# Down products ahead of the next up products in the first three places of a nine-unit expert round

## The reference, cut to what matters

```python
def expert_block(args):
    xb, e = args                       # up to 128 rows of one expert
    return (jax.nn.silu(xb @ w1[e]) * (xb @ w3[e])) @ w2[e]   # w1, w3: 1024x512, w2: 512x1024

y_rows = yb.reshape(-1, d)[dest] * wts.reshape(-1)[order][:, None]
return jnp.zeros_like(t).at[tok].add(y_rows)
```

## Time and profile before

| | us |
|---|---|
| median of 3 runs | 1163.68 |
| lowest, highest | 1163.40, 1164.49 |
| span of the profiled execution | 1160.8 |
| chain that ended last, by engine | PE 73%, DMA 14%, DVE 7%, ACT 3%, issue 2% |
| PE busy | 1093.8 (94% of the span) |
| DMA mean over the span | 241 GB/s |

### The profile page before, as it was taken

How to read it: one execution, slowest core, us unless ns; L and a number is a source line. 1 busy time by engine, 2 the same in 40 slices (tenths; PEclk the granted TensorE clock), 3 DMA queues, 4 the chain that set the end, 5 groups by cost and what they waited for, 6 DMA issues and landing times.

```text
span 1160.8 us, 16298 instructions
## 1 busy us (share of the span) xinstructions
PE 1093.8 (94%) x5691; PEld 700.4 (60%) x5691; DVE 562.6 (48%) x1011; ACT 317.0 (27%) x539; POOL 176.8 (15%) x255
## 2 busy tenths in 40 slices
PE   6999999989999999999999998899999899988985
PEld 4788888868667777778888777333333233322333
DVE  5776787745676788766564546221112111111114
ACT  4542322243334544342433242100000000000003
POOL 0000110000110323345000100122222122211220
PEclk9999999999999999999999998999999999999999
DMA  9423855720111222223132489989999999999975
GB/s 380 194 97 120 293 177 194 254 91 19 55 56 55 74 73 74 91 85 130 59 109 91 179 368 343 406 352 423 423 424 425 425 426 425 426 427 426 425 321 223
DMA packets 41981, 279.68 MB, mean 241 GB/s; under 512 B 7802, under 2 KB 8186, under 8 KB 30016
## 3 DMA queue, kind: packets, MB, share of 16 engines
q1 hardware_dynamic: 34496, 265.07, 57.3%
q0 software_dynamic: 7424, 13.80, 3.4%
HBM read 274.23 MB, written 13.40 MB: 248 GB/s over the span
## 4 chain that ended last, share of the span: by engine, by line
PE 73%; DMA 14%; DVE 7%; ACT 3%; issue 2%; SPq 0%; DVEq 0%; POOL 0%; ACTq 0%; POOLq 0%
PE psum L701 70%; DMA ering<-in_wb 8%; DMA ering<-in_wa 2%; DMA ada<-in_adaw 2%; DVE ring_lo L1538 1%; PE psum L717 1%; DVE amx L1809 1%; DVE sc L1798 1%; DMA xr<-token_rows,tabt 1%; ACT ring_hi L1235 1%; PE psum L1043 1%; PE psum L741 1%; DMA Hx<-in_xT 1%; DMA gat<-expert_rows 0%; ACT gth L1235 0%
## 5 line engine op out<-in xcount | busy, mean ns | idle before, releaser
L701 PE MATMUL psum<-ering,xs 128*64 128x512 f32 x1056 | 237.0, 599 | 18.7 <-DMA ering<-in_wb 9.1
L701 PE MATMUL psum<-Hhi,ring_hi 128*128 128x512 f32 x472 | 188.3, 399 | 0.1
L701 PE MATMUL psum<-Hlo,ring_hi 128*128 128x512 f32 x472 | 185.3, 393 | 0.2 <-DVE Hlo L1538 0.2
L701 PE MATMUL psum<-Hhi,ring_lo 128*128 128x512 f32 x472 | 183.1, 390 | 0.0
L701 PEld LDWEIGHTS psum<-ering,xs 128*64 128x64 f32 x1056 | 73.2, 137 | 160.9 <-issue 135.1
L1538 DVE TENSOR_TENSOR ring_lo<-ring,ring_hi 128x1024 fp32r<-128x1024 f32 x87 | 107.8, 1239 | 109.7 <-ACT ring_hi L1235 108.6
L1538 DVE TENSOR_TENSOR sg<-sg,psum 128x256 f32<-128x256 f32 x66 | 27.8, 421 | 236.8 <-ACT sg L1235 235.6
L701 PE MATMUL psum<-ering,at 128*64 128x512 f32 x528 | 119.5, 597 | 2.9 <-ACT at L1235 1.6
L1235 ACT ACTIVATE ring_hi<-ring 128x1024 fp32r<-128x1024 f32 x87 | 92.2, 1060 | 74.3 <-DMA ring<-in_stream 41.2
L701 PEld LDWEIGHTS psum<-Hhi,ring_hi 128*128 128x128 f32 x472 | 88.7, 188 | 22.7 <-issue 3.2
L701 PEld LDWEIGHTS psum<-Hhi,ring_lo 128*128 128x128 f32 x472 | 88.5, 188 | 19.7
(11 more groups left out here) (350 smaller groups left out, 1450.7 us busy)
## 6 DMA issues: line engine op xcount, KB each, us to landing
ering<-in_w SPq DMA_DIRECT2D x28, 2048.0 KB, 21.6
ering<-in_wb SPq DMA_DIRECT2D x28, 2048.0 KB, 27.8
ering<-in_wa SPq DMA_DIRECT2D x28, 2048.0 KB, 22.8
ring<-in_stream SPq DMA_DIRECT2D x87, 512.0 KB, 4.3
ada_ring<-in_stream SPq DMA_DIRECT2D x32, 512.0 KB, 3.7
ada<-in_adaw SPq DMA_DIRECT2D x4, 2048.0 KB, 10.8
Am<-decay_rows POOLq DMA_DIRECT2D x8, 512.0 KB, 4.5
gat<-expert_rows SPq DMA_DIRECT2D x4, 1024.0 KB, 8.0
```

The lines of the kernel that those rows point to most:

```text
L701: return nc.tensor.matmul(out, lhsT, rhs, start=start, stop=stop)
```

## The change

In the places with `a == 0` (q = 0, 1, 2) the test on `nh` goes, and `down`, `rows_out` and `rows_home_at` always stand ahead of the next unit's `up_and_gate`, `silu_times` and `gather`. The other six places, ScalarE and SyncE are as before.

```diff
--- before.py
+++ after.py
@@ -1194,8 +1194,11 @@
 
                                         up_and_gate(1, j, k + 1, here)
                                         tokens_in(1, k + 2)
-                                with pe.If(k >= nh):
+                                if a == 0:
                                     down(0, j, u + 1, here)
+                                else:
+                                    with pe.If(k >= nh):
+                                        down(0, j, u + 1, here)
                                 with pe.If(u + 1 < n):
 
                                     up_and_gate(0, (j + 1) % SLOTS, u + 2, then, True)
@@ -1206,10 +1209,11 @@
                                         act_turn(1, k + 1)
                                     with pe.If(u + 1 < n):
                                         tokens_in(0, u + 1)
-                                with pe.If(k < nh):
-                                    if heavy:
-                                        down(1, j, k + 1, here)
-                                    down(0, j, u + 1, here)
+                                if a > 0:
+                                    with pe.If(k < nh):
+                                        if heavy:
+                                            down(1, j, k + 1, here)
+                                        down(0, j, u + 1, here)
 
         for c in range(NCH):
             b = 4 + c % 2
@@ -2101,15 +2105,19 @@
                                     silu_times(1, k + 1)
                                     token_columns(1, k + 2)
                             with v.If(u < n):
-                                with v.If(k >= nh):
+                                if a == 0:
                                     rows_out(0, u + 1, u + 1)
+                                else:
+                                    with v.If(k >= nh):
+                                        rows_out(0, u + 1, u + 1)
                                 with v.If(u + 1 < n):
                                     silu_times(0, u + 2)
                                     token_columns(0, u + 1)
-                                with v.If(k < nh):
-                                    if heavy:
-                                        rows_out(1, k + 1, k + 1)
-                                    rows_out(0, u + 1, u + 1)
+                                if a > 0:
+                                    with v.If(k < nh):
+                                        if heavy:
+                                            rows_out(1, k + 1, k + 1)
+                                        rows_out(0, u + 1, u + 1)
 
         def rows_sum(c):
 
@@ -2263,15 +2271,19 @@
                                     with g_.If(k < nh):
                                         g_.wait_ge(xt_full[1], k + 2)
                                         gather(1, bass.ds(u * 2 + 2 * TRIO + 1, 1), k + 3)
-                                with g_.If(k >= nh):
+                                if a == 0:
                                     rows_home_at(0, bass.ds(u * 2, 1), u + 2)
+                                else:
+                                    with g_.If(k >= nh):
+                                        rows_home_at(0, bass.ds(u * 2, 1), u + 2)
                                 with g_.If(u + 1 < n):
                                     g_.wait_ge(xt_full[0], u + 1)
                                     gather(0, bass.ds(u * 2 + 6, 1), u + 2)
-                                with g_.If(k < nh):
-                                    if heavy:
-                                        rows_home_at(1, bass.ds(u * 2 + 1, 1), k + 2)
-                                    rows_home_at(0, bass.ds(u * 2, 1), u + 2)
+                                if a > 0:
+                                    with g_.If(k < nh):
+                                        if heavy:
+                                            rows_home_at(1, bass.ds(u * 2 + 1, 1), k + 2)
+                                        rows_home_at(0, bass.ds(u * 2, 1), u + 2)
 
     ctx.close()
```

## The result

The changed kernel takes 1168.53 us (median of 4 runs, 1167.96 to 1171.09), the kernel before 1163.54 beside it (4 runs, 1162.49 to 1164.49): 1.0056 times as long, interval [1.0041, 1.0072], 5.0 us slower by the medians, where +0.7 was forecast. The span of the profiled execution went from 1160.8 to 1166.1 us, +5.3.

A forecast was written before the change was run, and what follows sets the result against it. The expert stage was taken as bound by DMA, its weight stream; hole +0.5 and scatters +0.2 made span 1160.8 into 1161.5, so 1163.68 + 0.7 = 1164.4 us. The forecast's own range was 1163.3 to 1166.0, the overall range 1161.2 to 1167.7.

The forecast's parts named there:

- Scatters: In round 0, unit 1's eviction waits for unit 0's scatter, landing after 8.1 us, and delays unit 3's up: +0.2 (0 to 1.4).
- The late scatter as a rival: Unit 0's scatter lands late beside a full queue; at 11 us +3 and the hole +0.5, 1167.2 us; chance 0.11.
- the list of waits that the prediction counted: Eleven halves of up products on TensorE waiting for weight loads, 904.09 to 1060.28, taken to absorb PE's delay of rounds 1 and 2.
- The hole's own term: The early break in the weight stream moves back 10 us and lacks 5.4 to 6.0 against 5.2: +0.2 to +0.8, taken +0.5.
- slot 2's condition: Unit 5's `wa` and `wb` wait for unit 3's first up matmul, so go out at 766.17 instead of 761.17, taking the gain.
- three loads issued within a microsecond start faster: If these restart the stream after the hole faster than one load alone did, the low end of +0.2 to +0.8 is nearer.
- PE's delay: PE runs 4.0 us late in round 0 and 4.2 more in each of rounds 1 and 2; queued loads and waits absorb it.
- The reserve: Weight loads still queued at 817.33, the lowest point: 4.8 MB or 11 us, counting about 13 gathers and scatters; 4.0 fit.
- The gather: Now issued behind the scatter, near 762.8, landing at 770.9; `tokens_in` wants it at 771.9 with 0.8 us cover: costs nothing.
- Branches: A test and a code copy fall away at each changed place: taken as nothing, bounds -0.4 to 0.
- the ends -0.2 and +2.2: Lower and upper ends of the summed change, from +0.2 - 0.4 to +0.8 + 1.4, around the forecast +0.7.

The follow-up runs named there:

- run 3: The changed kernel with ten 128-column filler matmuls ahead of `act_turn` of unit 2 in round 0, shared buffer kept: 1166.17 us against 1162.31 for the kernel before.
- run 5: The changed kernel measured again, unaltered: 1167.52 us against 1162.22 for the kernel before.
- run 13: The changed kernel measured once more, unaltered, in the last set: 1169.22 us against 1162.78 for the kernel before.
- run 15: Down first in round 0 alone, shared buffer kept, without the third code copy: 1167.43 us against 1162.78 for the kernel before.
- run 1: The changed kernel with round 0 back in the old order, down first in rounds 1 and 2 only: 1163.06 us against 1162.31 for the kernel before.
- run 8: The kernel before with slot 2's wa and wb freed behind the up products at q = 0: 1161.82 us against 1162.22.
- run 12: The kernel before with a third copy of the code at q = 0 to 2, all in the old order: 1162.55 us against 1162.51.
- run 9: Down first in round 0 alone, unit 0's rows in their own buffer, no third code copy: 1163.93 us against 1162.51 for the kernel before.
- run 6: Down first in round 0 alone, unit 0's rows in their own buffer, with a third code copy: 1167.37 us, 1.0048 times the kernel before.
- run 2: The changed kernel with unit 0's rows in a buffer of their own: 1165.76 us against 1162.31 for the kernel before.
- run 7: Down first at q = 0 of round 0 only, own buffer, slot 2 freed early, third code copy there: 1167.62 us against 1162.22 for the kernel before.
- run 4: Down first in round 0 only, own buffer, slot 2 freed early, third code copy: 1168.39 us against 1162.31 for the kernel before.
- run 10: Run 9 with slot 2 freed early and GpSimd's gather ahead of the scatter: 1167.11 us against 1162.51 for the kernel before.
- run 11: Run 10 with down first only at q = 0 of round 0: 1161.68 us against 1162.51 for the kernel before.

## Why the prediction was wrong

**The step that failed** is "Scatters", the term "+0.2 (0 to 1.4)". It asked the right question, when VectorE's eviction of unit 1 is free against when its multiplications are wanted, and put both within 0.2 us; as up of unit 3 shows it, this wait cost 5.05 us in place of 0.2. Measured, the eviction was wanted at 756.5 (up of unit 2 at 749.71, + 6.97 + 0.53 - 0.69) and began at 759.45: 2.9 late. Of this,

- 0.2 was forecast;
- 1.7 is the landing, 9.8 us against the median of 8.1 taken. It was 9.5 to 9.8 in all five profiled executions of down first in round 0 with the shared buffer (after, runs 3, 5, 13 and 15). The range's upper end, 9.3, was below all of them. Behind it stood the assumption that the latency of before holds, although the new order keeps the weight queue full beside the scatter, where before it ran empty about 5 us after its issue. That a scatter does not stand behind the weights' backlog holds (9.8 us against 25.7 for a `wb` load), but it says nothing on how much longer a scatter takes beside a full queue;
- 1.0 is a smaller lead: PE came to `act_turn` of unit 1 2.3 us earlier than in the profiled execution of before, the scatter only 1.3 earlier. The prediction took one execution's offset between two engines for fixed: from `act_turn` of unit 1 to the scatter's issue it was 3.4 us there and 4.4 in the changed kernel, but over all 17 profiled executions it runs from 3.3 to 4.7, and it is 3.4 to 4.7 in the four with the old order in round 0 (before, runs 1, 8 and 12).

**A term was missing: the clock.** With the eviction 2.9 late PE was idle for 3.65 and the granted clock fell to 0.50. Read from the trace (no experiment parts the wait's share from the clock's), `act_turn` came 2.84 late and cost 0.26 more, down 1.95 more (5.43 to the next start instead of 3.48). So up of unit 3 came 2.84 + 0.26 + 1.95 = 5.05 later than the forecast order gives from 749.71 (762.61), and the rows show 767.66. The late scatter as a rival had price 3 at a landing of 11 us; it cost more at 9.8, because its price left out the clock and the smaller lead. The trace of before had a sign of the clock's term, in the list of waits that the prediction counted. Of its eleven halves of up products this one took 5.35 us and the others 3.65, those behind 2.05 and 2.19 us of waiting among them:

```profile
1039.48 5.35 PE L701 MATMUL psum<-ering,xs 128*64 128x512 f32 x16 [1.86 <-DMA ering<-in_wa]
```

The Trainium skill ("TensorE: Matmul & The Clock Gate", section "HAM oscillation — how this bites in real kernels") describes this for waits on a DMA, which make the next group of matmuls start at the lower clock. The traces agree, here behind waits on VectorE of 3.40 to 3.87 us, with 5.35 to 5.60 us in place of 3.65.

**The hole's own term was near.** It was "+0.5" (0.2 to 0.8). Without the scatter's wait the hole is 4.9, 5.1 and 4.5 us (runs 9, 6 and 2) against 5.2 in the profiled execution of before, so -0.1 to -0.7; but with the old order it is 4.2 and 4.5 in runs 1 and 12, against which the same holes are up to 0.9 longer, so the profiles show no more than that this term is small. `in_w` of unit 4 did go out early, and slot 2's condition did take the gain. That three loads issued within a microsecond start faster is not seen: from the first issue on the 6 us behind it lack 1.6 us against 425 GB/s in the changed kernel (three loads) and 1.5 before (one).

**PE's delay was absorbed, not quite for nothing.** In round 0 the stream did not run dry (the changed kernel lacks 0.2 us at 804 to 832). The reserve had been counted too high: GpSimd issued 10 gathers and scatters between 759.67 and 817.33, not 13, which leaves 4.0 MB or 9.4 us queued instead of 11, and still covers the 4.0. Run 1 gives +0.6 us (-1.0 to +2.2) for rounds 1 and 2. But the loads' waits, counted one by one in the earlier trace rows, gather into one of 4.4 us, and behind it the clock is low for part of unit 23's up products: from the last `wa` to their end 9.9 us (run 1) and 10.0 (run 2), 8.9 in the changed kernel, 8.7 before. A part of run 2's remaining loss may be that; how much can't be told within its interval, and the rest of it stays open.

**The gather** behind the scatter cost nothing, as forecast. That was not luck of the late PE: in run 9, where PE is on time, the gather went out at 763.13 and `tokens_in` began at 770.17 without a wait. It needs down first at q = 1, though: run 7, which has it at q = 0 only, wants the tokens 3.5 us earlier in its order and waits 5.60.

**Branches**: nothing showed, as taken.

The sum, measured on the two profiled executions: -0.1 to -0.7 for the hole itself and +5.05 for the eviction's wait with its clock give 4.4 to 5.0, and the hole did grow by 4.6 (3.3 and 3.5 in runs 5 and 13, the same kernel again). Of this 4.4 arrive at the last `wa`; the up products behind it add 0.2, and 0.7 more lie between 1068 us and the end of the span, which no row accounts for. Beside the sum, the ends -0.2 and +2.2 on 1163.68 give 1163.5 to 1165.9 and not the 1163.3 to 1166.0 that stand there; the result is outside either.

## What to carry to other kernels

When a step that waits for a DMA's landing is moved ahead of another on an engine, the slack is the difference of two engines' times and should be read from several places of the trace, and the latency taken from rows in which the queues beside it are as full as they will be. Price every new wait on TensorE with the slower clock of the group behind it: here 2.9 us of lateness cost 5.1. And where a stream of weights through a ring sets the end, a hole early in it can arrive at the end in full, as 4.4 of 4.6 us did here; closing it moved it in runs 4 and 10, and where PE kept up as well (run 11) the profile gained 1.8 us at the last load and the times nothing that is clear of the noise.

## What the runs showed of the hardware

- How long an indirect scatter of 128 half rows takes depends on what lies beside it, by more than the 7.6 to 9.3 of the earlier trace rows. Issued into the hole it landed after 4.0 us (run 9, unit 1: issued 761.01, GpSimd released at 765.00) or less (unit 1 in run 2: issued 761.66, VectorE released at 764.35), beside the emptying weight queue after 7.8, in the steady stream after 7.6 to 8.1 (the changed kernel, 765 to 905 us), and beside a full queue right behind two gathers after 9.5 to 9.8. A gather alone ahead gave 9.6 (run 10, unit 1), none 8.6 (run 4, unit 1). The two gathers stand ahead of unit 0's scatter in the old order too, so they alone don't make it late: read at GpSimd's next index copy, it took 7.5 to 8.6 us from its issue in the four profiled executions with the old order in round 0 (before, runs 1, 8 and 12) and 8.7 to 10.0 in the eleven with down first in which that copy waited for it. No experiment changed the gathers alone.

```profile
761.01 1.01 POOL L2239 DMA_INDIRECT expert_rows<-ysb,idx  x1 [0.91 <-POOL idx L2246]
...
765.00 0.18 POOL L2246 COPY idx<-tabd 128x1 uint32 x1 [0.81 <-DMA expert_rows<-ysb,idx]
```

- A TensorE that had been idle for 3.65 us was granted 0.50 (the changed kernel, 760 to 764), and behind 3.4 to 3.9 us of idle time (the changed kernel, runs 5, 13 and 15) 16 matmuls of 512 columns took 5.35 to 5.60 us instead of 3.65. They took 5.35 also behind a wait of 2.06 and one for ScalarE of 0.55 (run 10), behind fillers and a wait of 1.69 (run 3), and in the kernel before behind one of 1.86 (1039.48); behind 2.19 (before, 1024.04) and behind 0.80 and 0.55 they took 3.65. The length of the last wait alone doesn't tell which.
- A weight stream that ran empty starts slowly: the first 6 us from its first new load lack 1.4 to 1.6 us against 425 GB/s, whether one load is issued and the next 1.3 to 1.5 us later (before, runs 1, 8, 12) or three within 1 us (the changed kernel, runs 2, 3, 5, 6, 9, 13, 15).
- With 37 instead of 23 instruction packets (runs 4 and 6) the last of the sixteen increments of each weight load came 2.8 to 5.5 us behind the fifteenth from `w` of unit 20 on, and at most 1.1 in units 18 to 27 of all other runs; no experiment shows which causes which.
